# The last norm's scale and shift of the token rows moved from VectorE to GpSimd, in a two-layer encoder trunk with eight experts

## What is computed

```python
out, sc = mix_hgrn2(x, j, lower_bounds[layer], p, s_hgrn[j])
x = layer_norm(ALPHA * x + out, p['ln_c_g'][j], p['ln_c_b'][j])
moe = moe_swiglu(x, p['moe_router'][j], p['moe_w1'][j], p['moe_w3'][j], p['moe_w2'][j])
x = layer_norm(ALPHA * x + moe, p['ln_moe_g'][j], p['ln_moe_b'][j])
```

## Time and profile before

| | |
|---|---|
| median of 3 runs | 1492.17 us (1491.59 to 1493.68) |
| profiled execution, its own time | 1491.27 us |
| its span in the trace | 1489.3 us |
| TensorE (PE) busy | 1449.5 us, 97% |
| VectorE (DVE) busy | 1188.1 us, 80% |
| ScalarE (ACT) busy | 937.6 us, 63% |
| GpSimd (POOL) busy | 74.9 us, 5% |
| mean granted clock of TensorE | 0.993 |

### The profile page before, as it was taken

How to read it: one execution, slowest core, us unless ns; L and a number is a source line. 1 busy time by engine, 2 the same in 40 slices (tenths; PEclk the granted TensorE clock), 3 DMA queues, 4 the chain that set the end, 5 groups by cost and what they waited for, 6 DMA issues and landing times.

```text
span 1489.3 us, 28994 instructions
## 1 busy us (share of the span) xinstructions
PE 1449.5 (97%) x11160; PEld 1298.6 (87%) x11161; DVE 1188.1 (80%) x1611; ACT 937.6 (63%) x1236; POOL 74.9 (5%) x148
## 2 busy tenths in 40 slices
PE   8999998999999899999999999999999999999996
PEld 8998988999999899888788888888888888888884
DVE  6686888555445798877999998899989899898997
ACT  4563144533333596565778877688787887877873
POOL 8300000000000000000000000000000000000000
PEclk9999999999999999999999999999999999999999
DMA  9421005444444353226899999999999999999992
GB/s 282 144 86 35 4 3 156 142 142 148 156 135 146 100 167 119 84 69 249 299 385 395 409 388 398 335 405 383 370 398 339 410 378 362 398 343 410 382 357 73
DMA packets 162127, 371.71 MB, mean 250 GB/s; under 512 B 10184, under 2 KB 85872, under 8 KB 162032
## 3 DMA queue, kind: packets, MB, share of 16 engines
q1 hardware_dynamic: 159256, 361.13, 66.0%
q0 software_dynamic: 2160, 7.87, 1.9%
q10 hardware_dynamic: 616, 1.37, 0.2%
HBM read 360.63 MB, written 9.71 MB: 249 GB/s over the span
## 4 chain that ended last, share of the span: by engine, by line
PE 90%; DVE 6%; ACT 2%; issue 1%; DMA 0%; SPq 0%; DVEq 0%; ACTq 0%
PE bank L546 11%; PE bank L1218 11%; PE bank L1219 10%; PE bank L1220 10%; PE bank L548 10%; PE bank L547 10%; PE bank L1242 5%; PE bank L1244 5%; PE bank L1243 5%; PE bank L637 4%; PE bank L1227 1%; PE bank L978 1%; PE bank L753 1%; DVE wd_lo L1314 0%; PE bank L1277 0%
## 5 line engine op out<-in xcount | busy, mean ns | idle before, releaser
L2004 DVE TENSOR_TENSOR w_lo<-moe_ring,w_hi 128x1024 fp32r<-128x1024 f32 (+1 forms) x560 | 608.4, 1155 | 29.7 <-ACT w_hi L2731 29.7
L2731 ACT ACTIVATE w_hi<-moe_ring 128x1024 fp32r<-128x1024 f32 (+1 forms) x560 | 531.5, 1014 | 73.4 <-PE bank L1244 39.1
L1218 PE MATMUL bank<-w_hi,xe_hi 128*128 128x512 f32 (+1 forms) x768 | 288.2, 375 | 1.3 <-DVE w_lo L2004 1.3
L546 PE MATMUL bank<-in_hi,wd_hi 128*128 128x320 f32 x872 | 275.4, 316 | 10.8 <-DVE in_lo L1697 8.9
L1219 PE MATMUL bank<-w_hi,xe_lo 128*128 128x512 f32 (+1 forms) x768 | 285.9, 372 | 0.0
L1220 PE MATMUL bank<-w_lo,xe_hi 128*128 128x512 f32 (+1 forms) x768 | 285.4, 372 | 0.0
L1314 DVE TENSOR_TENSOR wd_lo<-arena,wd_hi 128x1024 fp32r<-128x1024 f32 x141 | 169.6, 1207 | 138.9 <-ACT wd_hi L2266 138.8
L548 PE MATMUL bank<-in_hi,wd_lo 128*128 128x320 f32 x880 | 274.8, 312 | 0.0
L547 PE MATMUL bank<-in_lo,wd_hi 128*128 128x320 f32 x872 | 271.7, 312 | 0.0
L2266 ACT ACTIVATE wd_hi<-arena 128x1024 fp32r<-128x1024 f32 (+1 forms) x140 | 145.8, 1048 | 156.8 <-PE bank L548 156.7
L546 PEld LDWEIGHTS bank<-in_hi,wd_hi 128*128 128x128 f32 x872 | 165.8, 190 | 13.8 <-issue 9.7
(11 more groups left out here) (413 smaller groups left out, 1705.0 us busy)
## 6 DMA issues: line engine op xcount, KB each, us to landing
moe_ring<-in_moe_w SPq DMA_DIRECT2D x216, 1024.0 KB, 8.6
moe_ring<-in_moe_w SPq DMA_DIRECT2D x64, 768.0 KB, 5.2
arena<-in_ffn_w SPq DMA_DIRECT2D x30, 1024.0 KB, 5.4
arena<-in_w_in_c SPq DMA_DIRECT2D x16, 1024.0 KB, 5.3
arena<-in_w_in_ab SPq DMA_DIRECT2D x12, 1024.0 KB, 5.8
arena<-in_w_out_ab SPq DMA_DIRECT2D x4, 1024.0 KB, 5.0
arena<-in_w_out_c SPq DMA_DIRECT2D x4, 1024.0 KB, 5.0
arena<-in_ffn_w SPq DMA_DIRECT2D x4, 768.0 KB, 4.3
```

The source lines that it names most:

```text
L546: pe.matmul(b[:, 0:T], w_[0][:, cols], x_hi, start=start, stop=False)
L1218: pe.matmul(b[:, 0:w], xe_hi[:, k, :], hi_[:, c0:c1], start=(k == 0), stop=False)
L2004: dve.tensor_tensor(w_lo[:, i % UNITS, 0:unit_words(i)], moe_unit(i), w_hi[:, i % UNITS, 0:unit_words(i)], ALU.subtract)\
L2731: act.activation(w_hi[:, i % UNITS, 0:unit_words(i)], moe_unit(i), ACT.Copy).then_inc(S("e_hi"), 1)
```

## The change

The six row instructions leave VectorE's program. They now stand in GpSimd's, at the head of the first expert, in the order multiply, add for each of the three row tiles. GpSimd waits first for the six writes of `xtok` by ScalarE (`xtok_done`), for the two groups of products in which TensorE reads the unscaled `xtok` (`e_features_full`, 2) and for both vectors (`ln_gb_in`). It waits for each multiply before the add of the same tile; the multiply of the next tile has no wait. The stores to `x_rows` move from behind units 14, 18 and 22 to behind 14, 19 and 24, those to `y_rows` from piece 22 to piece 23.

```diff
-ROW_UNITS, STORE_UNITS, BASE_PIECE, LN_PIECE = [8, 10, 12, 14, 16, 18], [14, 18, 22], 22, 33
+STORE_UNITS, BASE_PIECE, LN_PIECE = [14, 19, 24], 23, 33
...
-            def rows_scaled(i, a):
-
-                n = TILES[i][1]
-                if a == 0:
-                    dve.wait_ge(*at_count("ln_gb_in", 32))
-                    dve.tensor_tensor(xtok[0:n, i, :], xtok[0:n, i, :], ln_gb[0:n, 0, :], ALU.mult).then_inc(S("x_scaled"), 1)
-                else:
-                    dve.wait_ge(*at_count("x_scaled", i + 1))
-                    dve.tensor_tensor(xtok[0:n, i, :], xtok[0:n, i, :], ln_gb[0:n, 1, :], ALU.add).then_inc(S("x_whole"), 1)
...
-                        if i in ROW_UNITS:
-                            rows_scaled(*divmod(ROW_UNITS.index(i), 2))
...
+                        pool.wait_ge(*at_count("xtok_done", 6))
+                        pool.wait_ge(S("e_features_full"), 2)
+                        pool.wait_ge(*at_count("ln_gb_in", 32))
+                        for i, (_, rows) in enumerate(TILES):
+                            pool.tensor_tensor(xtok[0:rows, i, :], xtok[0:rows, i, :], ln_gb[0:rows, 0, :], ALU.mult).then_inc(S("x_scaled"), 1)
+                            pool.wait_ge(*at_count("x_scaled", i + 1))
+                            pool.tensor_tensor(xtok[0:rows, i, :], xtok[0:rows, i, :], ln_gb[0:rows, 1, :], ALU.add).then_inc(S("x_whole"), 1)
                         pool.wait_ge(*at_count("x_rows_in", 48))
```

## The result

The changed kernel takes **1496.50 us** (median of 9 runs, 1493.70 to 1497.84) against 1492.17 for the kernel before (nine runs as well, 1489.39 to 1493.68): a ratio of 1.0030, 95% interval 1.0021 to 1.0038. It is slower by 0.3%. The prediction was 1496.6, with a range from 1490.0 to 1501.5.

What follows compares the result with a forecast made beforehand. TensorE was taken to bound the kernel, waiting for VectorE only in the first expert. 5.9 us of lateness plus 0.4 for restarts minus 1.9 gave +4.4 on the median of 1492.17: 1496.6 us, range 1490.0 to 1501.5.

Steps and rivals of the forecast that it cites:

- What bounds: TensorE, busy for all 647.00 us of the later experts, so time lost in the first expert is not won back.
- What is taken away, 1.9 us: First expert: TensorE's waits for VectorE's `w_lo`, 1.5 us idle plus 0.4 for four restarts, the most to be gained.
- The disturbance: First expert: GpSimd and VectorE shut each other out for two-input reads, each while the other streams; 2 us per GpSimd instruction.
- Rival A: GpSimd holds reads only in short bursts and does not stop VectorE; all waits go, 1490.3 us; chance 0.20.
- B: Rival: a cheap GpSimd instruction, both inputs at the pace of one, t = 1.1; 1491.1 us; chance 0.09.
- C: Rival: a dear GpSimd instruction at the iota's pace, t = 4.0; 1508.6 us; chance 0.10, with anything above t = 2.6.
- The length, t = 2.0: One GpSimd row instruction, t, takes 2.0 us: two inputs of 1024 elements read one after the other.
- The sum: First expert: 5.9 us late at unit 9, plus 0.4 for restarts, minus 1.9 for waits gone, gives +4.4 us.
- 6t - 6.1: How late `w_lo` of unit 9 comes for TensorE, with t for one GpSimd instruction; 5.9 us at t = 2.0.
- My 0.4 for four restarts: First expert: four restarts of TensorE after new waits for `w_lo`, 0.11 us each, added to the lateness.
- +4.4: Forecast net change in us of the whole kernel, giving 1496.6 us from the median before.
- The clock: Risk that TensorE's granted clock falls while it idles between 719 and 729 us; at most some 1.5 us, none taken.

Runs made afterwards that it cites:

- Experiment 1: Changed kernel without the scale and shift of the token rows on either engine, stores kept in place: median 1488.53 us, 0.9978 of the kernel before.
- Experiments 1 to 3: Experiment 1; the same plus six GpSimd writes that read nothing (152.31 us from VectorE's first `xe_lo` to GpSimd's multiply in the second expert); experiment 3.
- experiment 5: Kernel before with only the `x_rows` and `y_rows` stores moved as in the change, rows still on VectorE: ratio 1.0001.
- experiment 3: Experiment 1 plus six one-input GpSimd multiplies of a 128x1024 tile: 152.29 us from VectorE's first `xe_lo` to GpSimd's multiply in the second expert.
- experiment 6: Changed kernel with GpSimd's second to sixth row instructions held back to later units and later stores: median 1496.13 us, ratio 1.0037.

## Why the prediction was right

*What bounds.* Right. Later experts kept TensorE busy for 647.00 of 647.00, and the 4.4 to 4.6 us lost in the first expert came out as 4.33 in the median.

*What is taken away, 1.9 us.* Too small. Experiment 1 gives 2.6 to 2.8. The idle time was read rightly; the restart was sized from how much longer one matmul is (0.11 us), while the whole stop costs 0.3.

*The disturbance.* Right, both ways, with VectorE getting one instruction between two of GpSimd's. Experiments 1 to 3 show that it is the reads and that nothing else in the change costs anything; experiment 5 clears the stores. Rival A is refuted by `w_lo` of 3.43 us, B and C by the hold. That each engine shuts the other out for its whole length holds only for the two-input instruction: with one input the hold was 0.84 of 2.8 us. The prediction used one number, t, for both.

*The length, t = 2.0.* The hold is 2.18; a whole instruction with VectorE idle for most of it takes 2.4, of which 0.19 passed beside the end of the first `xe_lo`. The Trainium skill's figure ("GPSIMD Engine Reference", section "3.1 Elementwise — side-by-side cycle accounting"), halved to 2.25 us as an estimate, was nearer than mine. The reasoning behind 2.0, two inputs at a one-input pace, was less sound than its result: experiment 3's one-input instruction is slower than the two-input one.

*The sum.* 6t - 6.1 with 2.18 gives 7.0 us at unit 9, and the trace has 16.57 us from unit 2 to 9 for 9.52, 7.05 late, where I had 5.9. My 0.4 for four restarts did not belong beside it: 6t - 6.1 goes from start to start, so whatever the first three stops cost is hidden in the next wait, and only what follows the last start comes on top, 0.2 us (7.24 in all, 159.53 - 152.29). So the added side was 7.2 for my 6.3, and 2.6 to 2.8 were taken away where I had 1.9. The two errors cancel, so +4.4 was met to within 0.2 us by luck, with two terms that were each off by 0.7 to 0.9 us. With only t put right it would have read 7.0 + 0.4 - 1.9 = +5.5. The forecast wait of TensorE, 5.9 us, looks met too by the 6.0 of the trace, but 5.9 was the lateness, which is 7.05.

*The clock.* Taking none of the risk was right here, and experiment 6 shows that the risk was real. TensorE was busy for 5.67 of 10 us between 720 and 730 (I had forecast under half), in four stops of 1.00 to 1.67 us, and its granted clock stayed at full speed, unlike ahead of the first expert and behind the stop of 3.0 us in experiment 6:

```profile
720.00:730.00 10.00, 5.67 (x23) 3.71 (x22) 10.00 (x4) 5.23 (x7) 9.84 (x4) 1.00 0.60 195
```

## What to carry to other kernels

Work moved from VectorE to GpSimd is not off VectorE if both read on-chip memory: here 1.14 us of VectorE's own time became 2.18 us of waiting, for five of the six instructions (the first fell into an idle gap of VectorE), at the one place where TensorE was waiting for VectorE already. Count the holds as if they were VectorE instructions, against the lead that VectorE has there, and put such work into real gaps of VectorE, on whichever engine. And when a step is put off, look for queued instructions, a store behind a wait above all, that hold an engine until it is done.

## What the runs showed that I had not expected

- GpSimd multiplies a 128x1024 fp32 tile by a constant in 2.8 us, longer than it needs for two tiles (2.4 with VectorE idle for most of it), but keeps VectorE from reading for only 0.84 us.
- Turns are not always one and one. Between two-input instructions of GpSimd VectorE got one `w_lo`; between one-input ones it got two, the second while GpSimd's instruction still ran but no longer held it. In experiment 6 a GpSimd instruction stood still from 764.63 to about 770 us behind a row of `w_lo`, and what decided that is open.
- Each stop of TensorE costs some 0.3 us beyond its idle time.
- Four stops of 1.00 to 1.67 us, one after the other, left the granted clock at full speed; one stop of 3.0 us was followed by some 3 us at about half of it.
